# Companion products inside the state steps of a delta rule (TensorE, fp32, one core)

## The reference, cut to what matters

```python
def step(state, xs):
    u_i, w_i, a_i, qd_i, kd_i, gl_i = xs
    v_new = u_i - einsum('bhcd,bhde->bhce', w_i, state)
    o = einsum('bhcd,bhde->bhce', qd_i, state) + einsum('bhij,bhje->bhie', a_i, v_new)
    state = state * gl_i[..., None, None] + einsum('bhcd,bhce->bhde', kd_i, v_new)
    return state, o
```

## Time and profile before

| What | Value |
|---|---|
| Median of 3 runs | 2014.56 us |
| Profiled execution | 2014.65 us, its span 2012.8 us |
| TensorE matmul busy | 1983.9 us, 99% |
| VectorE, ScalarE, GpSimd busy | 1581.3, 1217.1, 98.7 us |
| Stage of the state steps, layer 0 and layer 1 | 830.65 to 846.5 us and 1168.63 to 1184.46 us |

### The profile page before, as it was taken

The page is one execution under the profiler, slowest core; times in us unless marked ns, Lnnn a source line. Parts: engine busy times, 40 slices in busy tenths (PEclk is TensorE's granted clock), DMA queues, the critical chain, the costliest instruction groups (busy, mean ns, idle before and its releaser), DMA issues.

```text
span 2012.8 us, 30330 instructions
## 1 busy us (share of the span) xinstructions
PE 1983.9 (99%) x11699; PEld 1681.0 (84%) x11699; DVE 1581.3 (79%) x1632; ACT 1217.1 (60%) x1303; POOL 98.7 (5%) x163
## 2 busy tenths in 40 slices
PE   8999999999999999999999999999999999999997
PEld 7878888887888898888889888888888888888886
DVE  7787745778774569775458978999999998999997
ACT  6565534556554456544436646777777777777775
POOL 0300000030000000000000000000000000000000
PEclk9999999999999999999999999999999999999999
DMA  8326555632655554065556309999999999999995
GB/s 302 117 67 215 192 195 185 203 128 62 217 189 195 195 200 148 22 215 188 189 168 209 106 1 364 362 358 372 361 364 363 361 365 363 364 364 364 367 361 198
DMA packets 154088, 481.06 MB, mean 239 GB/s; under 512 B 14608, under 2 KB 41728, under 8 KB 153856
## 3 DMA queue, kind: packets, MB, share of 16 engines
q1 hardware_dynamic: 150064, 465.46, 64.5%
q0 software_dynamic: 3920, 14.16, 2.0%
HBM read 477.48 MB, written 2.10 MB: 238 GB/s over the span
## 4 chain that ended last, share of the span: by engine, by line
PE 90%; DVE 7%; ACT 1%; issue 1%; DMA 1%; POOL 0%; SPq 0%; DVEq 0%; POOLq 0%; ACTq 0%
PE G L694 18%; PE G L696 18%; PE G L695 18%; PE Sp L694 5%; PE Sp L696 5%; PE Sp L695 5%; PE G L1185 3%; PE G L721 3%; PE G L1186 2%; PE G L681 1%; DVE ring_lo L2169 1%; PE G L676 1%; PE G L677 1%; PE Sp L1185 1%; PE G L1570 1%; DVE e_lo L2945 1%
## 5 line engine op out<-in xcount | busy, mean ns | idle before, releaser
L2945 DVE TENSOR_TENSOR e_lo<-e_raw,e_hi 128x1408 fp32r<-128x1408 f32 x384 | 601.2, 1619 | 19.9 <-ACT e_hi L2092 17.6
L2092 ACT ACTIVATE e_hi<-e_raw 128x1408 fp32r<-128x1408 f32 x384 | 524.0, 1382 | 153.1 <-DMA e_raw<-in_moe_w_gate 57.6
L2169 DVE TENSOR_TENSOR ring_lo<-ring,ring_hi 128x2048 fp32r<-128x2048 f32 (+2 forms) x171 | 383.5, 2254 | 182.3 <-ACT ring_hi L1655 180.9
L1655 ACT ACTIVATE ring_hi<-ring 128x2048 fp32r<-128x2048 f32 (+1 forms) x179 | 335.6, 1884 | 229.4 <-PE G L696 135.7
L694 PE MATMUL G<-e_hi,xgTh 128*128 128x512 f32 (+1 forms) x768 | 291.8, 380 | 0.1
L696 PE MATMUL G<-e_hi,xgTl 128*128 128x512 f32 (+1 forms) x768 | 288.3, 375 | 0.0
L695 PE MATMUL G<-e_lo,xgTh 128*128 128x512 f32 (+1 forms) x768 | 285.3, 372 | 0.0
L694 PE MATMUL G<-ring_hi,xT 128*128 128x512 f32 (+2 forms) x488 | 190.9, 391 | 0.0
L696 PE MATMUL G<-ring_hi,xT 128*128 128x512 f32 (+2 forms) x488 | 187.4, 384 | 0.0
L695 PE MATMUL G<-ring_lo,xT 128*128 128x512 f32 (+2 forms) x488 | 187.2, 384 | 0.0
L696 PEld LDWEIGHTS G<-e_hi,xgTl 128*128 128x128 f32 x768 | 144.0, 188 | 25.1
(11 more groups left out here) (464 smaller groups left out, 3374.7 us busy)
## 6 DMA issues: line engine op xcount, KB each, us to landing
e_raw<-in_moe_w_gate SPq DMA_DIRECT2D x128, 704.0 KB, 5.9
e_raw<-in_moe_w_up SPq DMA_DIRECT2D x128, 704.0 KB, 5.9
e_raw<-in_moe_w_down SPq DMA_DIRECT2D x128, 704.0 KB, 5.9
ring<-in_w_in SPq DMA_DIRECT2D x48, 1024.0 KB, 5.1
ring<-in_w_mlp_up SPq DMA_DIRECT2D x32, 1024.0 KB, 5.2
ring<-in_w_mlp_down SPq DMA_DIRECT2D x32, 1024.0 KB, 4.8
ring<-in_w_out SPq DMA_DIRECT2D x16, 1024.0 KB, 4.9
ring<-in_ffn_w_gate SPq DMA_DIRECT2D x22, 512.0 KB, 3.8
```

The lines of the kernel that those rows point to most:

```text
L1655: nc.scalar.activation(ring_hi[:, n % H, 0:m], ring[:, n % R, 0:m], ACT.Copy).then_inc(w_hi.sem, 1)
L2092: nc.scalar.activation(e_hi[:, u, :], e_raw[:, u, :], ACT.Copy).then_inc(w_hi.sem, 1)
L2169: v.tensor_tensor(ring_lo[:, n % R, cs], ring[:, n % R, cs], ring_hi[:, n % H, cs].bitcast(F32), ALU.subtract).then_inc(w_lo.sem, 1)
L2945: v.tensor_tensor(e_lo[:, u, :], e_raw[:, u, :], e_hi[:, u, :].bitcast(F32), ALU.subtract).then_inc(w_lo.sem, 1)
```

## The change

by_state and in_chunk are dissolved into single products, state_product(n, h) and chunk_product(tb, half, h). less_state and to_state get a companion chunk: before each head's own product they issue one of the companion's. Dilated values and transposes change places with them. On ScalarE the evacuation of PT2[:, 1] moves ahead of the wait for `o_full`. No instruction is added or removed in number.

```diff
-            def by_state(ns):
-
-                for h in range(H2):
-                    for n in ns:
-                        tb, half = n // 2, n % 2
-                        pe.matmul(Sp[half * CHUNK:(half + 1) * CHUNK, tb, h * P:(h + 1) * P], CV[:, h, n * CHUNK:(n + 1) * CHUNK], STATE[n % 2][:, h, :],
-                                  start=(h == 0), stop=False, skip_group_check=True)
-
-            def less_state(n):
+            def state_product(n, h):
+                tb, half = n // 2, n % 2
+                pe.matmul(Sp[half * CHUNK:(half + 1) * CHUNK, tb, h * P:(h + 1) * P], CV[:, h, n * CHUNK:(n + 1) * CHUNK], STATE[n % 2][:, h, :],
+                          start=(h == 0), stop=False, skip_group_check=True)
+
+            def less_state(n, beside=None):
                 tb, half = n // 2, n % 2
                 for h in range(H2):
+                    if beside is not None:
+                        state_product(beside, h)
                     last = pe.matmul(G[half * CHUNK:(half + 1) * CHUNK, 0, h * P:(h + 1) * P], WTs[:, half, tb * 4 + h, :], STATE[n % 2][:, h, :],
                                      start=True, stop=True, skip_group_check=True)
                 last.then_inc(pe2d.sem, 1)
 
-            def to_state(n):
+            def chunk_product(tb, half, h):
+                both = HALVES[half]
+                return pe.matmul(Sp[both, tb, h * P:(h + 1) * P], AC[both, tb * 4 + h, :], DT[both, tb * 4 + h, :],
+                                 start=(tb == 0 and half == 0 and h == 0), stop=True, skip_group_check=True)
+
+            def to_state(n, beside=None):
                 tb, half = n // 2, n % 2
                 rows = slice(half * CHUNK, (half + 1) * CHUNK)
                 pe.wait_ge(d2pe.sem, d2pe.next("pe"))
                 for h in range(H2):
+                    if beside is not None:
+                        other = chunk_product(beside // 2, beside % 2, h)
                     last = pe.matmul(T[0][:, h * P:(h + 1) * P], KD[rows, tb * 4 + h, :], DT[rows, tb * 4 + h, :], start=True, stop=True)
+                if beside is not None and beside % 2:
+                    other.then_inc(o_full.sem, 1)
                 last.then_inc(pe2d.sem, 1)
...
             less_state(1)
-            by_state([1])
-            to_state(1)
             dilated_values(0)
+            to_state(1, 0)
             dilated_transposes(1, 0)
             pe.wait_ge(d2pe.sem, d2pe.next("pe"))
-            less_state(2)
-            in_chunk(0)
-            to_state(2)
+            less_state(2, 1)
             dilated_transposes(1, 1)
+            to_state(2, 1)
+            dilated_values(1)
             pe.wait_ge(d2pe.sem, d2pe.next("pe"))
-            less_state(3)
-            dilated_values(1)
+            less_state(3, 2)
+            for h in range(H2):
+                state_product(3, h)
             token_transposes(XN, 0, xn_block)
-            by_state([2, 3])
             pe.wait_ge(d2pe.sem, d2pe.next("pe"))
-            in_chunk(1)
+            for h in range(H2):
+                for half in range(2):
+                    last = chunk_product(1, half, h)
+            last.then_inc(o_full.sem, 1)
...
             evac(PT2[:, 0, :, :])
             dilated_exps(1)
             evac(PT2[:, 0, :, :])
+            evac(PT2[:, 1, :, :])
...
                 if tb == 0:
-                    evac(PT2[:, 1, :, :])
                     met(0)
                     block_evac(0)
```

## The result

The changed kernel took 2024.6 us (median of 5 runs, 2022.21 to 2027.13) against 2014.56 us before: ratio 1.0048, 95% interval 1.0037 to 1.0059. The direction was forecast, the size was not: 10.0 us lost, not 5.7, and the forecast's range ended at 2022.0.

What follows compares the result with a forecast made beforehand. TensorE was taken as the bound, with work in 99% of the span, losing time where its stream waits or stretches. Layer 0's +3.02 and layer 1's +2.64 made +5.7 us on 2014.56: 2020.2 us, range 2018.4 to 2022.0.

Steps and rivals of the forecast that it cites:

- (a): Layer 1: to_state(1) with companion ends 1.99 us later, so L2817 starts 1175.89 and less_state(2) 1.70 us later, at 1176.63.
- (b): Layer 1: L2810 ends at 1178.50, so to_state(2) starts 1.59 us later, at 1178.56 instead of 1176.97.
- (c): Layer 1: to_state(2) takes 1.99 us more, dilated values follow, so less_state(3) starts 3.66 us later, at about 1182.63.
- (e): Layer 1: ScalarE's squares and ring_hi copies run late; L1681 starts at about 1186.12, L676 at 1187.48, 3.02 us later.
- The four prices of 0.20, 0.16, 0.20 and 0.21 us: Start-to-start times of a head's matmuls in to_state with companion: together 0.77 us, 1.99 us extra a call.
- Rival B: In to_state with companion both shapes run side by side, so it lasts as long as alone: 2013.2 us, chance 0.09.
- rival C: In to_state with companion only the shape change itself costs, weights being loaded ahead: 0.62 us a head, 2017.8 us, chance 0.05.
- One argument against B: Both kinds of shape change in the earlier trace have different row halves, and yet show no overlap.
- Step (f): Layer 1: squares of block 1, normalisation and ring_lo copies come 2.64 us later, so the layer ends 2.64 us later.
- 1.3 and twice 0.4: Forecast's own error: 1.3 us in all from matmul starts, 0.4 a layer where ScalarE or TensorE binds in (e).
- Against it: the clock is full in all slices: Argument against the clock falling: it was full everywhere, also in both layers' stages that already have such changes.
- rival D: Clock falls to 1.2 GHz in the thinned stretch, about 5 us a layer more: 2030 us, chance 0.03.

Runs made afterwards that it cites:

- e3: Changed kernel, but companions in less_state only; to_state runs alone, in-chunk products of block 0 in one group: 2013.46 us, ratio 0.9995.
- e9: Changed kernel, but shapes alternate in layer 0 only; in layer 1 each key product is cut into two column halves: 2021.08 us, ratio 1.0026.
- e10: Changed kernel, but shapes alternate in layer 1 only; in layer 0 each key product is cut into two column halves: 2018.62 us, ratio 1.0015.
- e1: Changed kernel, but each key product of to_state is cut into two of 64*64, so no change of shape is left: 2013.78 us, ratio 0.9994.
- e2: Changed kernel, but in a to_state with companion all four companions come first, then the four key products: 2016.05 us, ratio 1.0007.

## Why the prediction was right and wrong

The stage of layer 1 began 7.76 us later after the change (1175.65 against 1167.89). With that taken off, its steps came where they were put (lines by their numbers before):

| Step of the sum | Predicted start | Measured start - 7.76 |
|---|---|---|
| (a) L2817 behind to_state(1) | 1175.89 | 1175.92 |
| (a) less_state(2) | 1176.63 | 1176.66 |
| (b) to_state(2) | 1178.56 | 1178.60 |
| (c) less_state(3) | 1182.63 | 1182.68 |
| (e) L1681 | 1186.12 | 1186.01 |
| (e) L676 | 1187.48 | 1187.47 |

The four prices of 0.20, 0.16, 0.20 and 0.21 us gave 0.77 a head and 0.77 was measured; a call was to last 3.1 us (2.88 to the last start) and lasted 3.17. The changed kernel's stage at full clock is 3.01 us longer; 3.02 was forecast. Rival B is refuted by the same rows (that loads for the other row half run ahead does not hold from one shape to the other), rival C by the second matmul of each group. That less_state takes a companion for nothing is shown by the two products that start together and by e3. One argument against B was weaker than it looked, though. The groups of the earlier trace rows are pairs that run in both row halves at once, so there the half that a new group goes to was never free; the groups of the changed kernel leave one half empty, and they show that this does not help. Step (f) came true as well. The last group of TensorE's products, first before, then after:

```profile
1999.71 0.47 PE L1635 MATMUL G<-YBh,PmT 128*128 128x512 f32 x1 [1.78 <-DVE YBl L3011]
```

```profile
2010.17 0.47 PE L1638 MATMUL G<-YBh,PmT 128*128 128x512 f32 x1 [1.87 <-DVE YBl L3014]
```

It is 10.46 us late, of which 7.76 were there ahead of layer 1's stage: 2.70 for layer 1, forecast 2.64. Between the profiled executions lie 10.9 us (2025.55 - 2014.65): 5.7 as summed, 5.04 of clock in layer 0, and some tenths at the start and the end, where the last five matmuls ran at the half level (0.56 to 0.63 us each instead of 0.40). The range was somewhat narrower than its own terms: 1.3 and twice 0.4 are 2.1 us, and 1.8 was taken. It would have missed either way.

What failed is the step "Against it: the clock is full in all slices, also in layer 0's and 1's stages that already have such changes", which put the clock at nothing in the sum, and with it the 0.03 given to rival D. D's size, 5 us in a layer, was right where the fall came: 5.04 us in layer 0. It came in one layer of the two, and not in both as D's 2030 has it. The changes in the stage before are single ones between long groups of one shape, and nothing in the trace of before showed what 14 of them in two calls do to the clock. From "no fall at a few changes" I went to "no fall at many", over a distance that no row covered. The clock should have been a term of the sum with two ends, 0 and about 5 us a layer; that range would have reached 2030 and held the result. The runs support the link to the changes well, but do not explain it fully. With 0, 1 or 3 changes a call no profile shows a fall in the companions' calls; with 7 in both calls four profiled stages of six had one, with 7 in one call one of two. All five began 2.4 to 3.4 us after the start of the first call that alternates. And e9 and e10 follow the layer in which the changes stand. What in the thinned stretch (the alternating calls, with a start every 0.16 to 0.21 us instead of every 0.11) the chip reacts to is open, and so is why one execution falls and the next does not. I tried nothing that keeps the pauses and fills them, nor the same length of stage without them.

Busy shares don't warn of it. Over the layer-1 stage of the changed kernel TensorE's matmul rows cover 17.56 of 19.60 us, since the length of a row runs on through the pause. Nor do the weight loads settle it. They cover 13.17 of 19.60 us there (67%), where the clock stayed full. In e1's layer 0, without a change of shape and at full clock, they cover 10.90 of 15.80 (69%). And the fall of e1 came behind a stretch in which they covered 4.73 of 5.85 (81%).

## What to carry to other kernels

Put beside each other only matmuls of one array shape, rows and columns both; then different halves do run at once and a companion is free (e1, e3). If the shapes differ, cut the larger product to the smaller shape (e1) or keep each shape in one group (e2's stages cost 0.73 us over before, e3's nothing). To put the companions' group behind the urgent products was not tried. Where a change thins TensorE's stream for a few microseconds, carry the clock as a term of its own with both levels as ends, however full it was before.

## What the runs showed of the hardware that I had not expected

In layer 0 the granted clock fell within the first call that alternates, 2.5 us after its start (834.35 to 836.8), and stayed down over 13.7 us although the matmul rows of that stretch leave no gap (13.70 us of 13.70). The same program on the same chip had runs from 2021.51 to 2027.91 us, while e2 with one change a call stayed within 2015.12 to 2017.04 in ten of eleven: the alternation cost steadiness as well as time in these runs. And matmuls of one shape but different output halves pass each other. So it is not quite so that TensorE runs its instructions in the order of the program: the first dilated value (L1250), written behind all eight matmuls of less_state(1), starts before the sixth of them.

```profile
832.44 0.73 PE L1411 MATMUL G<-ARENA 128*64 128x128 f32 x5 [0.36 <-DVE ARENA L2823]
...
832.90 0.27 PE L1250 MATMUL G<-ARENA,PT 128*64 128x64 f32 x1
833.00 0.27 PE L1411 MATMUL G<-ARENA 128*64 128x128 f32 x1
```
